# A feed-forward kernel whose gate and up products go from three 256-column steps to one of 512 and one of 256

## The chip, the cores and the metric

The kernel runs on one core of one Trainium2 chip. The metric is the device time of one execution in microseconds (us). TensorE multiplies, VectorE and ScalarE do the elementwise work, SyncE issues the weight transfers, GpSimd a few small ones.

## The reference, cut to what matters

A transformer stack over 256 tokens of 1024 channels, all in float32: a first block with four kinds of token mixing and a feed-forward network, then a second block of two layers, one with a short convolution and one with differential attention, each followed by a feed-forward network and a gated per-layer embedding. The change lies in the three feed-forward networks. The first is

```python
def conv_glu_ffn(h, w_up, conv_w, conv_b, w_down):
    u = causal_dwconv(h @ w_up, conv_w) + conv_b
    gate, up = jnp.split(u, 2, axis=-1)
    return (jax.nn.silu(gate) * up) @ w_down
```

where h is an RMS norm of x, the convolution has 3 taps along the tokens, and gate and up have 2816 channels each. The other two are the same without the bias, and their result is normalised before it is added to x.

## The kernel before, in words

**Precision.** Every float32 operand of a large product is split in two float32r parts: ScalarE rounds it (the high part), VectorE subtracts that from the original (the low part). A product is then the sum of three: high weights by high activations, high weights by low activations, low weights by high activations. The activations of a feed-forward stage are h_hi and h_lo, 8 chunks of 128 channels by 256 tokens.

**Weights.** They come as a stream of 161 blocks of 128 x 2048 elements (1 MB) in the order of use. The ring has 3 slots. For block n SyncE loads raw (once the low part of block n - 3 is made), ScalarE writes w_hi (once TensorE has used block n - 3, whose slot it takes: `act.wait_ge(block_used, n - 2)`), VectorE writes w_lo. `ahead(n)` splits block n + 2. All four engines have their order written out by hand, and wait for each other by counting semaphores.

**A feed-forward stage** (FFN 0, 1, 2; `ffn(f, p)` on each engine) has 33 blocks, called b0 to b32 here. The 2816 hidden channels are done in 11 pairs of 128-channel tiles. Pair q has a gate block, an up block and a down block:

- b0, b1: gate 0 and up 0 (written chunk by chunk as h arrives, `columns_by_chunk`, banks 4 and 5); b2, b3: gate 1, up 1 (banks 6, 7); b4, b5: gate 2, up 2 (banks 4, 5); b6: down 0
- then in a loop of four, two pairs each (`triple`): b7, b8: gate 3, up 3, b9: down 1; b10, b11: gate 4, up 4, b12: down 2; and so on to b28, b29 (gate 10, up 10) and b30 (down 8); at the end b31, b32: down 9 and down 10.

A gate or up block (`columns`) is 48 products: for each of 2 tiles and 8 chunks the three products above, 256 columns each, so that a block's result fills one PSUM bank (2 x 256 columns). The pairs take turns: odd ones use banks 6 and 7, even ones 4 and 5. Banks 0 to 3 hold the sum of the down products (`channel_rows`, 48 products a block). In `triple` TensorE waits for `gate_read` of the pair two before (same bank), for `up_read` likewise, and for `hidden_split` before the down block.

**What VectorE and ScalarE do for pair q.** VectorE reads the gate bank, multiplied by the norm's factor r_x (`read`, L2375, 128 x 512 in one instruction); ScalarE makes the last tap of the convolution (L1536, twice, with a bias in FFN 0 alone); VectorE adds the two older taps (L2357, L2361, twice each); ScalarE takes SiLU (L1545). Up goes the same way without SiLU. VectorE multiplies the two to `hidden` (L2389), ScalarE makes its high part (L1551, `hid_part`), VectorE its low part (L2393), which is `hidden_split`. In the loop VectorE's order is: w_lo of the down block, read gate, taps, w_lo of the next gate block, read up, taps, hidden, w_lo of the next up block, low part of hidden. ScalarE's is: w_hi of the down block, last tap of gate, w_hi of the next gate block, SiLU, last tap of up, w_hi of the next up block, high part of hidden. The splits are L1173 (w_hi) and L1782 (w_lo).

At the start of a stage VectorE's order is: read gate 0, split b4, taps, read up 0, split b5, taps and hidden, read gate 1, split b6, low part of hidden 0, taps, read up 1, split b7, taps and hidden, read gate 2, low part of hidden 1, taps, split b8, read up 2, taps and hidden, low part of hidden 2. ScalarE's: split b4, tap of gate 0, split b5, SiLU and tap of up 0, split b6, high part of hidden 0, tap of gate 1, split b7, SiLU and tap of up 1, split b8, high part of hidden 1, and so on.

Behind FFN 0 comes the residual (`add_residual`, L2271) and the next projection; behind FFN 1 and 2 the squares of the result (L1219) and the per-layer embedding.

Of the kernel before, what the change touches and what calls it, by code (L numbers as in the profile page):

```python
# [10 lines left out]
R = mybir.dt.float32r  # L11
# [5 lines left out]
P = 128  # L17
# [58 lines left out]
for _name, _n in (("fox_b_f", 4), ("gdn_dt", 4), ("gdn_a_log", 4), ("fox_on", 64),  # L76
# [18 lines left out]
    "grams": ("decay_logs", "qk_gram", "decay_turned", "m_turned"),  # L95
    "constants": ("eps_set", "ones_set", "zeros"),
# [9 lines left out]
def build(nc, weights, small_in, x_in, masks_in, ident_in, channel_in, row_in, w_gk_in, p_in, table_in,  # L106
          onehot_in, flip_in, out):
    bias_dram = nc.dram_tensor("bias_by_distance", (N_HEADS, N_DIST), F, kind="Internal").ap()
    with ExitStack() as ctx:
# [16 lines left out]
        h_hi = sb("h_hi", [P, KC, TOK], R)  # L126
        h_lo = sb("h_lo", [P, KC, TOK], R)
# [114 lines left out]
        hidden = place([P, 2, TOK])  # L242
        y_scaled = (y_gate, y_up, z_gate, z_up)
# [152 lines left out]
        def _(pool):  # L396
# [18 lines left out]
            pool.wait_ge(sem("bias_rows"), 1)  # L415
# [11 lines left out]
        def _(pe):  # L427
# [7 lines left out]
            def columns(n0, slot, bank, operand, channel_major=True, middle=(), chunks=None):  # L435
# [4 lines left out]
                for f in range(2):  # L440
# [3 lines left out]
                    for k in range(KC):  # L444
# [9 lines left out]
                        else:  # L454
# [6 lines left out]
                            last = mm(o, a_lo[:, k, tok], ws_hi, False, k == KC - 1)  # L461
                last.then_inc(block_used, 1)
# [513 lines left out]
            def ffn(f, p):  # L976
# [43 lines left out]
            for j in range(4):  # L1020
                n = STEP["sc_out"] + j
                if j == 3:
                    pe.wait_ge(sem("table_loaded"), 32)
                    pe.wait_ge(sem("sc_gc"), 4)
                    mm(PS[0:N_HEADS, 5, 0:N_DIST], table, onehot).then_inc(sem("bias_by_head"), 1)
# [37 lines left out]
            last.then_inc(sem("bias_flipped"), 1)  # L1063
# [12 lines left out]
            def turn_weights(h):  # L1076

                if h == 0:
                    pe.wait_ge(sem("bias_copied"), 1)
# [76 lines left out]
        def _(act):  # L1156
# [365 lines left out]
            def ffn(f, p):  # L1522
# [15 lines left out]

                def gate(q):
# [41 lines left out]
                up(2)  # L1581
# [28 lines left out]
            act.wait_ge(sem("bias_by_head"), 1)  # L1610
# [1163 lines left out]
```

## Time and profile before

| | |
|---|---|
| median of 3 runs | 1098.3 us (1098.29 to 1100.12) |
| the profiled execution | 1100.87 us, span 1099.1 us |
| TensorE matmul | 1063.6 us busy (97%), 9090 instructions |
| VectorE | 804.0 us (73%) |
| ScalarE | 595.6 us (54%) |
| mean granted TensorE clock | 0.992 |
| read from memory | 172.2 MB, 158 GB/s over the span |

The matmul records overlap (one lasts 0.28 us and the next starts 0.12 us later), so the pace is read from start to start, or from the chain of waits. The granted clock is 1.00 at 2.4 GHz and 0.50 at 1.2 GHz. FFN 0 runs from about 212 to 404 us, FFN 1 from 505 to 697 and FFN 2 from 860 to 1053.

### The profile page before, as it was taken

Reading aid. Unit: us, or ns where it says so; the run is one execution under the profiler, and the core shown is the slowest. Engines: PE = TensorE matmul, PEld = TensorE weight load, DVE = VectorE, ACT = ScalarE, POOL = GpSimd, SP = SyncE. Lnnn points to the kernel's source line nnn. Section 1 sums busy time; section 2 is a strip of 40 time slices with the busy share of each in tenths; the row PEclk is TensorE's granted clock in tenths of the full one; section 3 lists DMA queues with packets and bytes.
Section 4 is the critical chain, followed back from the end, with each engine's and each line's share of the span. In section 5 each row is a group of like instructions: output and inputs, shape, how many; then the busy total and the mean of one; then the engine's idle time right before and its main releaser. Section 6 shows DMA issues by size and latency. Waiting matters only on the chain.

```text
span 1099.1 us, 22114 instructions
## 1 busy us (share of the span) xinstructions
PE 1063.6 (97%) x9090; PEld 1039.6 (95%) x9090; DVE 804.0 (73%) x1129; ACT 595.6 (54%) x781; POOL 5.3 (0%) x15
## 2 busy tenths in 40 slices
PE   6999999999999999999999999999998999999996
PEld 6999998999999999998999999989998899999995
DVE  5965678777877786757978777778763787877775
ACT  6652446465555464445555545676665555454563
POOL 0000000000000000000000000000000000000000
PEclk9999999999999999999999999999999999999998
DMA  8421232454555545553655554445343255555431
GB/s 327 156 78 39 78 119 93 150 195 151 191 189 188 195 155 187 183 201 121 202 186 177 194 194 168 154 154 167 141 154 114 92 187 184 193 189 191 153 115 39
DMA packets 25714, 174.23 MB, mean 159 GB/s; under 512 B 3069, under 2 KB 3349, under 8 KB 5296
## 3 DMA queue, kind: packets, MB, share of 16 engines
q1 hardware_dynamic: 25088, 171.57, 45.1%
q0 software_dynamic: 560, 1.70, 0.5%
q8 instruction: 51, 0.84, 0.3%
q14 instruction: 15, 0.12, 0.0%
HBM read 172.20 MB, written 1.06 MB: 158 GB/s over the span
## 4 chain that ended last, share of the span: by engine, by line
PE 71%; DVE 7%; ACT 3%; issue 2%; DVEq 0%; ACTq 0%
PE PS L429 39%; PE PS L466 32%; DVE w_lo L1782 3%; ACT w_hi L1173 2%; DVE arena L2357 1%; ACT arena L1536 1%; DVE arena L2361 1%; DVE arena L2375 1%; DVE x L2304 0%; PE PS L1087 0%; DVE arena L2298 0%; DVE h_lo L1795 0%; DVE arena L2300 0%; DVE arena L2389 0%; DVE arena L2350 0%
## 5 line engine op out<-in xcount | busy, mean ns | idle before, releaser
L1782 DVE TENSOR_TENSOR w_lo<-raw,w_hi 128x2048 fp32r<-128x2048 f32 x158 | 361.1, 2287 | 69.8 <-ACT w_hi L1173 68.1
L429 PE MATMUL PS<-h_hi,w_hi 128*128 128x256 f32 x1248 | 355.5, 285 | 2.6 <-DVE w_lo L1782 2.5
L429 PE MATMUL PS<-h_lo,w_hi 128*128 128x256 f32 x1248 | 353.1, 283 | 0.0
L429 PE MATMUL PS<-h_hi,w_lo 128*128 128x256 f32 x1248 | 353.1, 283 | 0.0
L1173 ACT ACTIVATE w_hi<-raw 128x2048 fp32r<-128x2048 f32 x158 | 300.7, 1905 | 86.2 <-PE PS L466 45.5
L429 PEld LDWEIGHTS PS<-h_hi,w_hi 128*128 128x128 f32 x1248 | 239.3, 192 | 4.3 <-issue 3.9
L429 PEld LDWEIGHTS PS<-h_lo,w_hi 128*128 128x128 f32 x1248 | 239.3, 192 | 0.3 <-issue 0.2
L429 PEld LDWEIGHTS PS<-h_hi,w_lo 128*128 128x128 f32 x1248 | 239.4, 192 | 0.0
L466 PE MATMUL PS<-act_hi,w_hi 128*128 128x256 f32 x720 | 202.2, 282 | 1.2 <-DVE act_lo L1812 1.2
L466 PE MATMUL PS<-act_hi,w_lo 128*128 128x256 f32 x720 | 202.3, 282 | 0.0
L466 PE MATMUL PS<-act_lo,w_hi 128*128 128x256 f32 x720 | 199.7, 283 | 0.0
L1536 ACT ACTIVATE arena<-arena,channel 128x256 f32<-128x256 f32 x132 | 63.9, 531 | 153.4 <-DVE arena L2375 153.4
L466 PEld LDWEIGHTS PS<-act_hi,w_hi 128*128 128x128 f32 x720 | 136.6, 190 | 2.7 <-DVE act_lo L1812 1.4
L466 PEld LDWEIGHTS PS<-act_hi,w_lo 128*128 128x128 f32 x720 | 135.2, 188 | 0.1
L466 PEld LDWEIGHTS PS<-act_lo,w_hi 128*128 128x128 f32 x720 | 133.5, 188 | 0.2
L466 PE MATMUL PS<-h_hi,w_hi 128*128 128x256 f32 (+1 forms) x344 | 97.7, 296 | 17.5 <-ACT h_hi L1190 14.2
L2357 DVE SCALAR_TENSOR_TENSOR arena<-arena,channel 128x255 f32<-128x255 f32 x132 | 58.0, 480 | 69.1 <-ACT arena L1536 69.1
L466 PE MATMUL PS<-h_hi,w_lo 128*128 128x256 f32 (+1 forms) x344 | 95.9, 291 | 0.0
L466 PEld LDWEIGHTS PS<-h_hi,w_hi 128*128 128x128 f32 (+1 forms) x344 | 67.9, 197 | 20.0 <-issue 10.5
L466 PE MATMUL PS<-h_lo,w_hi 128*128 128x256 f32 (+1 forms) x344 | 81.5, 291 | 0.2
L429 PE MATMUL PS<-arena 64*64 64x64 f32 (+8 forms) x1018 | 68.7, 256 | 2.9 <-DVE arena L2157 1.7
L429 PEld LDWEIGHTS PS<-arena 64*64 64x64 f32 (+7 forms) x1018 | 58.8, 155 | 10.9 <-issue 4.5
(304 smaller groups left out, 1304.0 us busy)
## 6 DMA issues: line engine op xcount, KB each, us to landing
raw<-weights SPq DMA_DIRECT2D x158, 1024.0 KB, 4.9
arena<-masks_in SPq DMA_DIRECT2D x1, 1856.0 KB, 14.7
raw<-weights SPq DMA_DIRECT2D x2, 512.0 KB, 5.9
x<-x_in SPq DMA_DIRECT2D x4, 256.0 KB, 7.4
arena<-bias_by_distance POOLq DMA_DIRECT2D x1, 1024.0 KB, 6.2
result<-x SPq DMA_DIRECT2D x4, 256.0 KB, 2.1
arena<-p_in POOLq DMA_DIRECT2D x2, 256.0 KB, 4.2
row<-row_in SPq DMA_DIRECT2D x1, 326.0 KB, 10.8
```

Source lines behind the costliest of these rows:

```text
L429: return pe.matmul(o, lhs, rhs, start=start, stop=stop)
L466: return pe.matmul(o, lhs, rhs, start=start, stop=stop, skip_group_check=True)
L1173: act.activation(w_hi[:, slot, :], raw[:, slot, :], ACT.Copy).then_inc(hi_ready, 1)
L1536: ins = act.activation(dst[:, c, :], src[:, c, :], ACT.Identity, scale=w, bias=b)
L1782: tt(w_lo[:, slot, :], raw[:, slot, :], w_hi[:, slot, :].bitcast(F), ALU.subtract).then_inc(lo_ready, 1)
L2357: stt(y[:, c, 1:TOK], src[:, c, 0:TOK - 1], channel[:, bass.ds(col(1) + c, 1)], y[:, c, 1:TOK], ALU.mult, ALU.add).then_inc(ready[0], 1)
L2361: ins = stt(y[:, c, 2:TOK], src[:, c, 0:TOK - 2], channel[:, bass.ds(col(0) + c, 1)], y[:, c, 2:TOK], ALU.mult, ALU.add)
L2375: tt(z, pair(bank), units(r_x[:, 0:TOK], 2), ALU.mult).then_inc(done, 1)
```

## The change

In the gate and up blocks of pairs 1 to 10 the high and low activations lie side by side, and the high weights are multiplied by both in one product of 512 columns; the low weights by the high activations are added to the first half. A tile thus fills one bank and a block two banks: columns 0 to 255 hold two of the three sums, columns 256 to 511 the third. All gate blocks use banks 6 and 7, all up blocks 4 and 5. ScalarE copies the second halves of both banks to `low` in SBUF (128 x 512), VectorE adds them to the first halves (128 x 512), and then multiplies by r_x. There is one buffer `low` for gate and up. Pair 0 keeps the old form; its up bank is read right behind its gate bank. The layout of h and TensorE's part come first below. Some semaphores used once are shared (`once`), to make room for `low_copied` and `parts_added`.

```diff
-        h_hi = sb("h_hi", [P, KC, TOK], R)
-        h_lo = sb("h_lo", [P, KC, TOK], R)
+        h_both = sb("h_both", [P, KC, 2, TOK], R)
+        h_hi, h_lo = h_both[:, :, 0, :], h_both[:, :, 1, :]
...
+        low = place([P, 2, TOK])
...
+            def wide_columns(n0, slot, bank):
+                block_ready(n0)
+                for f in range(2):
+                    o = PS[:, bank + f, :]
+                    for k in range(KC):
+                        at = k * 256 + f * P
+                        add(o, w_hi[:, slot, at:at + P], h_both[:, k, :, :].rearrange("p b n -> p (b n)"), k == 0)
+                        last = add(o[:, 0:TOK], w_lo[:, slot, at:at + P], h_hi[:, k, :], False, k == KC - 1)
+                last.then_inc(block_used, 1)
...
-                columns(n0 + 2, slot(2), 6, (h_hi, h_lo))
-                columns(n0 + 3, slot(3), 7, (h_hi, h_lo))
+                wide_columns(n0 + 2, slot(2), 6)
+                pe.wait_ge(sem("gate_read"), PAIRS * f + 1)
+                pe.wait_ge(sem("up_read"), PAIRS * f + 1)
+                wide_columns(n0 + 3, slot(3), 4)
...
-                    bank = 6 if odd else 4
-                    pe.wait_ge(sem("gate_read"), pairs_done)
-                    columns(n, slot(at), bank, (h_hi, h_lo))
-                    pe.wait_ge(sem("up_read"), pairs_done)
-                    columns(n + 1, slot(at + 1), bank + 1, (h_hi, h_lo))
+                    pe.wait_ge(sem("gate_read"), pairs_done + 1)
+                    wide_columns(n, slot(at), 6)
+                    pe.wait_ge(sem("up_read"), pairs_done + 1)
+                    wide_columns(n + 1, slot(at + 1), 4)
```

On ScalarE:

```diff
+                def low_part(bank, n_used, q, part):
+                    act.wait_ge(block_used, n_used)
+                    if part or not isinstance(q, int) or q > 1:
+                        act.wait_ge(sem("parts_added"), 2 * q + (2 * (PAIRS - 1) * f + part - 2))
+                    act.activation(low, PS[:, bank:bank + 2, TOK:512], ACT.Copy).then_inc(sem("low_copied"), 1)
...
-                def up(q):
+                def up(q, n_used=None):
                     act.wait_ge(sem("gate_convolved"), q + (PAIRS * f + 1))
                     act.activation(s_gate, y_gate, ACT.Silu).then_inc(sem("gate_silu"), 1)
+                    if n_used is not None:
+                        low_part(4, n_used, q, 1)
                     act.wait_ge(sem("up_read"), q + (PAIRS * f + 1))
...
                     split_of(n_base + 2, step, i)
+                    low_part(6, n_base + 1 + step * i, q, 0)
                     gate(q)
                     split_of(n_base + 3, step, i)
-                    up(q)
+                    up(q, n_base + 2 + step * i)
...
                 hid_part(0, 0)
+                low_part(6, n0 + 3, 1, 0)
                 gate(1)
                 ahead(n0 + 5)
-                up(1)
+                up(1, n0 + 4)
                 ahead(n0 + 6)
+                low_part(6, n0 + 5, 2, 0)
                 hid_part(1, 1)
```

On VectorE:

```diff
+                def read_wide(z, bank, done, q, n_used, part):
+                    dve.wait_ge(block_used, n_used)
+                    dve.wait_ge(sem("low_copied"), 2 * q + (2 * (PAIRS - 1) * f + part - 1))
+                    tt(z, PS[:, bank:bank + 2, 0:TOK], low, ALU.add).then_inc(sem("parts_added"), 1)
+                    dve.wait_ge(sem("parts_added"), 2 * q + (2 * (PAIRS - 1) * f + part - 1))
+                    tt(z, z, units(r_x[:, 0:TOK], 2), ALU.mult).then_inc(done, 1)
+                    dve.wait_ge(done, q + (PAIRS * f + 1))
...
                 read(z_gate, 4, sem("gate_read"), 0, n0 + 1)
+                read(z_up, 5, sem("up_read"), 0, n0 + 2)
                 ahead(n0 + 2)
                 gate(0)
-                read(z_up, 5, sem("up_read"), 0, n0 + 2)
...
-                read(z_gate, 6, sem("gate_read"), 1, n0 + 3)
+                read_wide(z_gate, 6, sem("gate_read"), 1, n0 + 3, 0)
```

All further reads of the stage become `read_wide` in their places, with bank 6 for gate and 4 for up.

## Rows read from the trace of the kernel before

**Rows 1.** Busy time by stretch: us, then busy (instructions) of each engine, PEclk, DMA
```profile
247.40:277.45 30.05, 28.98 (x241) 28.62 (x239) 22.23 (x31) 16.26 (x18) 0.00 (x0) 1.00 0.41 137
277.45:387.00 109.55, 109.55 (x913) 109.55 (x914) 82.97 (x98) 56.95 (x59) 0.00 (x0) 1.00 0.55 192
```
**Rows 2.** Chain that ended last, in order of time: start, us, what
```profile
224.32 23.05 PE PS L429 x192
...
387.08 11.53 PE PS L466 x96
...
405.01 12.13 PE PS L466 x96
...
680.17 15.85 PE PS L466 x132
```
**Rows 3.** Timeline of VectorE, FFN 0: start, us, instruction, idle before it
```profile
261.80 2.29 DVE L1782 TENSOR_TENSOR w_lo<-raw,w_hi 128x2048 fp32r<-128x2048 f32 x1 [1.11 <-ACT w_hi L1173]
264.00 0.68 DVE L2375 TENSOR_TENSOR arena<-PS,arena 128x512 f32<-128x512 f32 x1
266.29 0.88 DVE L2357 SCALAR_TENSOR_TENSOR arena<-arena,channel 128x255 f32<-128x255 f32 x2 [1.60 <-ACT arena L1536]
...
270.31 0.68 DVE L2375 TENSOR_TENSOR arena<-PS,arena 128x512 f32<-128x512 f32 x1
...
277.22 0.68 DVE L2393 TENSOR_TENSOR act_lo<-arena,act_hi 128x512 fp32r<-128x512 f32 x1
...
280.02 0.68 DVE L2375 TENSOR_TENSOR arena<-PS,arena 128x512 f32<-128x512 f32 x1
```
**Rows 4.** Timeline of VectorE, FFN 1, the reads L2375
```profile
557.59 0.69 DVE L2375 TENSOR_TENSOR arena<-PS,arena 128x512 f32<-128x512 f32 x1
...
563.62 0.68 DVE L2375 TENSOR_TENSOR arena<-PS,arena 128x512 f32<-128x512 f32 x1
...
573.12 0.68 DVE L2375 TENSOR_TENSOR arena<-PS,arena 128x512 f32<-128x512 f32 x1
```
**Rows 5.** Timeline of TensorE: first and last of five products of 512 columns
```profile
59.69 0.38 PE L466 MATMUL PS<-gd_hi,level_masks 128*128 128x512 f32 x1
...
60.57 0.38 PE L466 MATMUL PS<-gd_lo,level_masks 128*128 128x512 f32 x1
```
**Rows 6.** Timeline of VectorE, two additions, the second waiting for the first
```profile
215.65 0.68 DVE L1802 TENSOR_TENSOR arena<-xn 128x512 f32<-128x512 f32 x1
216.36 0.69 DVE L1804 TENSOR_TENSOR arena<-arena,xn 128x512 f32<-128x512 f32 x1
```
**Rows 7.** Timeline of ScalarE, a read of 512 columns from PSUM
```profile
694.61 0.60 ACT L1219 ACTIVATE xn<-PS 128x512 f32<-128x512 f32 x1 [0.42 <-PE PS L466]
```
**Rows 8.** Timeline of VectorE, start and end of FFN 0
```profile
227.47 0.68 DVE L2375 TENSOR_TENSOR arena<-PS,arena 128x512 f32<-128x512 f32 x1
...
236.87 0.69 DVE L2389 TENSOR_TENSOR arena<-arena 128x512 f32<-128x512 f32 x1
237.48 0.68 DVE L2375 TENSOR_TENSOR arena<-PS,arena 128x512 f32<-128x512 f32 x1
...
248.35 0.68 DVE L2375 TENSOR_TENSOR arena<-PS,arena 128x512 f32<-128x512 f32 x1
...
400.07 0.75 DVE L2271 TENSOR_TENSOR x<-x,PS 128x256 f32<-128x256 f32 x2 [1.01 <-PE PS L466]
```
**Rows 9.** Busy time by stretch, behind the short convolution; columns as in rows 1
```profile
501.00:517.70 16.70, 14.34 (x102) 14.04 (x103) 13.33 (x25) 9.59 (x16) 0.00 (x0) 0.90 0.30 94
...
502.00:503.00 1.00, 0.00 (x0) 0.00 (x0) 0.96 (x3) 0.30 (x1) 0.00 (x0) 1.00 0.88 156
...
505.00:506.00 1.00, 1.00 (x8) 1.00 (x7) 1.00 (x3) 0.72 (x2) 0.00 (x0) 0.59 0.28 115
```
**Rows 10.** Timeline of ScalarE, start of FFN 0
```profile
241.69 1.92 ACT L1173 ACTIVATE w_hi<-raw 128x2048 fp32r<-128x2048 f32 x1 [2.34 <-PE PS L429]
243.51 0.61 ACT L1545 ACTIVATE arena<-arena 128x512 f32<-128x512 f32 x1
```

More of the change, by code:

```diff
@@ L95 @@
     "grams": ("decay_logs", "qk_gram", "decay_turned", "m_turned"),
+    "bias_by_act": ("bias_rows", "bias_copied", "lambda_exps"),
+    "bias_by_pe": ("bias_by_head", "bias_flipped"),
     "constants": ("eps_set", "ones_set", "zeros"),
@@ L414, in _ @@
             pool.dma_start(p_tok, p_in[0]).then_inc(sem("p_loaded"), 16)
-            pool.wait_ge(sem("bias_rows"), 1)
+            pool.wait_ge(*once("bias_rows"))
             pool.dma_start(bias_dram, bias_row).then_inc(sem("bias_stored"), 16)
@@ L1024, in _ @@
                     pe.wait_ge(sem("sc_gc"), 4)
-                    mm(PS[0:N_HEADS, 5, 0:N_DIST], table, onehot).then_inc(sem("bias_by_head"), 1)
+                    mm(PS[0:N_HEADS, 5, 0:N_DIST], table, onehot).then_inc(once("bias_by_head")[0], 1)
                 pe.wait_ge(sem("sc_hidden"), j + 1)
@@ L1062, in _ @@
                 last = mm(PS[:, b, :], flip, bias_rev[:, 2 * b:2 * b + 2, :].rearrange("p h n -> p (h n)"))
-            last.then_inc(sem("bias_flipped"), 1)
+            last.then_inc(once("bias_flipped")[0], 1)
             def logits(h):
@@ L1078, in turn_weights @@
                 if h == 0:
-                    pe.wait_ge(sem("bias_copied"), 1)
+                    pe.wait_ge(*once("bias_copied"))
                 if h == 6:
@@ L1580, in ffn @@
                 gate(2)
-                up(2)
+                up(2, n0 + 6)
                 act.wait_ge(block_used, n0 + 7)
@@ L1609, in _ @@
                 ahead(STEP["sc_out"] + j)
-            act.wait_ge(sem("bias_by_head"), 1)
-            act.activation(bias_row, PS[0:N_HEADS, 5, 0:N_DIST], ACT.Copy).then_inc(sem("bias_rows"), 1)
+            act.wait_ge(*once("bias_by_head"))
+            act.activation(bias_row, PS[0:N_HEADS, 5, 0:N_DIST], ACT.Copy).then_inc(once("bias_rows")[0], 1)
             squares_of_y(2, 0, STEP["sc_out"] + 4)
@@ L1701, in _ @@
             ahead(a0 + 2)
-            act.wait_ge(sem("bias_flipped"), 1)
-            act.activation(flat(bias_t), PS[:, 0:4, :].rearrange("p b n -> p (b n)"), ACT.Copy).then_inc(sem("bias_copied"), 1)
+            act.wait_ge(*once("bias_flipped"))
+            act.activation(flat(bias_t), PS[:, 0:4, :].rearrange("p b n -> p (b n)"), ACT.Copy).then_inc(once("bias_copied")[0], 1)
             act.wait_ge(sem("lambda_sums"), 1)
-            act.activation(lam[:, 0:2], lam[:, 0:2], ACT.Exp).then_inc(sem("lambda_exps"), 1)
+            act.activation(lam[:, 0:2], lam[:, 0:2], ACT.Exp).then_inc(once("lambda_exps")[0], 1)
             ahead(a0 + 3)
@@ L2395, in triple @@
                 def triple(q, n_base, step, i, odd):
-                    bank = 6 if odd else 4
                     split_of(n_base + 2, step, i)
-                    read(z_gate, bank, sem("gate_read"), q, n_base + 1 + step * i)
+                    read_wide(z_gate, 6, sem("gate_read"), q, n_base + 1 + step * i, 0)
                     gate(q)
                     split_of(n_base + 3, step, i)
-                    read(z_up, bank + 1, sem("up_read"), q, n_base + 2 + step * i)
+                    read_wide(z_up, 4, sem("up_read"), q, n_base + 2 + step * i, 1)
                     up(q)
@@ L2419, in ffn @@
                 gate(1)
-                read(z_up, 7, sem("up_read"), 1, n0 + 4)
+                read_wide(z_up, 4, sem("up_read"), 1, n0 + 4, 1)
                 ahead(n0 + 5)
                 up(1)
-                read(z_gate, 4, sem("gate_read"), 2, n0 + 5)
+                read_wide(z_gate, 6, sem("gate_read"), 2, n0 + 5, 0)
                 hid_part(1, 1)
@@ L2429, in ffn @@
                 ahead(n0 + 6)
-                read(z_up, 5, sem("up_read"), 2, n0 + 6)
+                read_wide(z_up, 4, sem("up_read"), 2, n0 + 6, 1)
                 up(2)
@@ L2531, in lambda_minus @@
             def lambda_minus():
-                dve.wait_ge(sem("lambda_exps"), 1)
+                dve.wait_ge(*once("lambda_exps"))
                 link(tt(lam[:, 2:3], lam[:, 1:2], lam[:, 0:1], ALU.subtract))
@@ L2556, in head @@
                 if h == 0:
-                    dve.wait_ge(sem("bias_copied"), 1)
+                    dve.wait_ge(*once("bias_copied"))
                 for m in range(2):
```

## The prediction

> **What bounds the kernel now.** I read the busy table by stretch first [rows 1]. In the first feed-forward stage (FFN 0) TensorE is busy all the time from 277.45 to 387.00 us; VectorE works 82.97 of those 109.55 us and ScalarE 56.95. A block of 48 products is 5.76 us (96 of them took 11.53 [rows 2], 120 ns each), and a lap (one pair's gate block, up block and one down block) 17.28 us of TensorE. So in the steady part TensorE sets the time, and VectorE, with 13.1 us of work in a lap, seems to have 24% to spare. From 247.40 to 277.45 it is different: TensorE idles only 1.07 us, but VectorE shows waits of its own. There it is catching up, and its reads of gate 3 and gate 4 start 16.02 us apart [rows 3] while TensorE needs 17.28. This is the number that matters most: 16.0 us is the length of VectorE's lap when TensorE doesn't hold it up. It is longer than its 13.1 us of work, because inside a lap it waits twice for ScalarE's last taps (once 1.60 us, at 266.29). In FFN 1, where the tap has no bias, the lap is 15.53 us (557.59 to 573.12 [rows 4]). The cover over VectorE's chain is thus 1.3 us a lap in FFN 0 and 1.7 in FFN 1 and 2, not 4.
>
> **TensorE's part.** Sixty blocks (20 in each of three FFNs; pair 0 keeps the old form) change from 48 products of 256 columns to 16 of 512 and 16 of 256. The columns streamed are the same number; 16 starts are saved. Four steps between 512-column products take 60.57 - 59.69 = 0.88 us, 220 ns each [rows 5], where a 256-column one takes 120. A block goes from 5.76 to 16 x (220 + 120) = 5.44 us. If TensorE stayed the bound: 60 x 0.32 = 19.2 us saved, lap 17.28 - 0.64 = 16.64. Bounds: 16 x (213 + 120) = 5.33, if 512 columns at the granted 2.4 GHz (213 ns) cost nothing else, and 5.76, no gain, at twice the 256-column step. I take the row of the same width. The Trainium skill (TensorE: Matmul & The Clock Gate, Back-to-back issue gap) gives N/2.4 + 2.5 ns, 216 ns for 512 columns and 109 for 256; the rows show 220 and 120, and by the rule a block would take 5.20 us. Neither matters if VectorE takes over.
>
> **VectorE's lap.** Each wide block is read in two steps in place of one: add bank halves to ScalarE's copy, wait for that on its own semaphore, multiply. The multiply costs what the read did. The add is one more 128x512 operation; two such, the second waiting for the first, start 0.71 us apart [rows 6]. I take 0.72; the lower bound is 0.61 (back to back without a wait, 236.87 to 237.48 [rows 8]), the upper 0.87 if the two register-fed waits ahead of it show. Two adds make 1.44 us: the lap becomes 16.0 + 1.44 = 17.44 us in FFN 0 and 15.53 + 1.44 = 16.97 in FFN 1 and 2. Both are above 16.64. VectorE becomes the bound, and TensorE waits for w_lo of the up block, 0.3 to 0.8 us a lap. The copies are in time in this regime: ScalarE reads 512 columns from PSUM in 0.60 us [rows 7], two copies a lap take it from 57 to about 65 of 109.55 us busy, the up copy fits behind SiLU while VectorE splits the next gate block, and the gate copy behind the split of the next down block.
>
> **The start of each FFN.** Here lies most of the price. All wide gate blocks now use banks 6 and 7 and all wide up blocks 4 and 5, so block b4 (gate 2) may not start before gate 1 is read, b5 (up 2) not before up 1 is read. Before, these had banks of their own. VectorE's order puts these reads late. In the clock of FFN 0:
> Up 0 is read right behind gate 0 (227.47 [rows 8]) in place of after gate 0's taps: moved, not added, and b3 finds bank 4 and 5 read at 228.9. The product of pair 0 is made at 236.87 as before. ScalarE queues hid_part(0) (0.54) and then the copy (0.60) behind it, so the add starts at 237.46 + 0.05 + 1.2 = 238.8, the multiply ends at 240.2. TensorE, which starts b2 at 224.3 [rows 2], finished b3 at 224.3 + 2 x 5.44 = 235.2: it idles 5.0 us.
> b4 would run to 245.7. To that comes the clock. In the 16.70 us from 501.00 TensorE was busy for 14.34, with nothing in 502 to 503, so it stood still 2.4 us; the mean granted clock there was 0.90, which is 3.3 us at 0.50 (1.2 GHz), and it fell in 505 to 506 (0.59), after the work had resumed [rows 9]. 3.3 us at half speed lose some 1.6 us of streaming, and an idle twice as long should lose more: I take 2.0, the bounds are 0 and 3.2. End of b4: 247.7.
> Now ScalarE's queue: the split of b7 waits for b4, whose slot it takes (before at 241.69, when b4 ended, then SiLU [rows 10]). 1.9 for the split, 0.55 SiLU, 0.6 copy of up 1, only then VectorE's add and multiply, 1.4: b5 may start at 252.2. A second idle of 4.5 us, again with 2.0 for the clock; b5 ends at 259.7. ScalarE then splits b8 (1.9), copies gate 2 (0.6), VectorE adds and starts to multiply (0.7): 263.0. Before, gate 2 was read at 248.35.
> From there to the read of gate 3 it was 264.00 - 248.35 = 15.65 us [rows 8, 3]; two more adds make it 17.1, less 1.0 because the wait for a w_hi split (1.11 at 261.80 [rows 3]) has gone, TensorE being far ahead of it: gate 3's multiply at 279.1, 15.1 us late. Without the clock's part it would be 11.1.
> The Trainium skill (Perfetto Trace Analysis, Matmuls, under Optimizing Tensor Performance) speaks against this change in the same lines that speak for it: larger products are more efficient, but independent groups should rotate through different PSUM banks so that reading one overlaps the next. The trace before agrees as far as it can: with four rotating banks TensorE stands still 1.07 us from 247.40 to 277.45 [rows 1]. By the half on larger products alone the sum would be -19.2 us.
>
> **Steady part and tail.** FFN 0: pair 10's gate is multiplied at 279.1 + 7 x 17.44 = 401.2. Behind it the last down block needs pair 10's hidden_split: 0.72 (the up's add) + 6.31 (264.00 to 270.31, gate to up) + 6.91 (270.31 to 277.22, up to hidden's low part [rows 3]) + 0.68 = 14.6 us, then 5.76: end at 421.6. Before: 387.08 + 3 x 5.76 = 404.4 [rows 2]. That is +17.2. The next projection waits for VectorE's split of b34, the second block behind this FFN: it started at 405.01 [rows 2], 0.6 us after the end and 4.9 after the residual's first update (400.07 [rows 8]). Now that update waits for b33's split, which comes some 3.3 us behind the last hidden low part (ScalarE's table load and its own split of 1.9 are ahead of it, an estimate): 401.2 + 14.6 + 3.3 + 4.9 = 424.0, +19.0 for FFN 0 in all.
> FFN 1: gate 3 was read at 557.59, now 572.7; + 7 x 16.97 = 691.5. Tail: 0.72 + 6.03 (557.59 to 563.62) + 6.70 (the 6.91 less the 0.21 by which 563.62 to 573.12 is shorter than 270.31 to 280.02 [rows 3, 4]) + 0.68 + 5.76 = 19.9: 711.4, against 680.17 + 17.28 = 697.45 [rows 2]. +13.9. Behind it the squares follow the banks as before, nothing added. FFN 2 the same.
> Sum: 19.0 + 2 x 13.9 = 46.8 us. The profiled execution took 1100.87 us (span 1099.1), which gives 1147.7; the median of the runs is 1098.3, 2.6 lower, which gives 1145.1 us. The h_hi/h_lo layout and the shared semaphores (bias_by_act, bias_by_pe) move no instruction, and a 256-column operand stays contiguous: nothing, and no cover is needed.
>
> **Rivals.**
> (a) As the main case, but the clock stays up: 6 x 2.0 = 12 us less, 1133. For it: [rows 9] is one case, and the clock fell only 2 us after the work had resumed. Against: both idles are twice as long as the one that did it.
> (b) The stalls cost more: 3.2 us for the clock in each of six (+7), and the register-fed waits show, 0.15 on each add (7 laps x 2 x 3 x 0.15 = +6): 1158. For it: the idle of 1.60 us at 266.29, in the loop, is longer than the two taps that it waits for. Against: VectorE's sequencer can run ahead during a 2.28 us split.
> (c) The start hides: TensorE is let go earlier than I read the queue, and only six adds (4.3 us) shift gate 3. FFN 0: +4.3 + 7 x (17.44 - 17.28) - 2.6 (the last gate's read to the end: 23.0 before, 20.4 now) + 1.8 = +4.6; FFN 1, 2: 4.3 - 7 x 0.31 - 3.1 = -1.0 each: 1101. Against: the waits are in the code (gate_read at pairs_done + 1), and the copy stands behind hid_part(0).
> (d) The other side: TensorE stays the bound and the product's saving shows, 1098.3 - 19.2 = 1079. One mechanism decides: VectorE's lap below 16.64, that is an add that costs under 0.32 us in FFN 0 (0.55 in FFN 1, 2), or a VectorE that reads the bank earlier. A 128x512 operation takes 0.68 us in every row, so the row speaks against it, and the start's idles would have to vanish too.
> That the change doesn't do what it says is no case: banks, copies and products are all in the diff.
>
> **How the numbers follow.** Main (as summed, 1139 to 1151): 0.50. (a) 0.15. (b) 0.26. (c) 0.05. (d) 0.04. Predicted time 1145. The range runs from below (a), 1128 (adds at the lower bound, 0.11 x 42 = 4.6 less), to 1162 above (b); with the cases outside it 0.15 stay out. A measurement of this kernel tells some 0.2% (2.2 us) from nothing. Faster: (d), 0.04; same: part of (c), 0.02; slower: 0.94.
>
> **What would show it.** TensorE idle before b4 and b5 of each FFN, 4 to 5 us each, released by the multiply behind read_wide, with PEclk at 0.50 soon after; steps of 220 ns between 512-column products; gate multiplies 17.4 us apart in FFN 0 and 17.0 in FFN 1 and 2; TensorE waiting for w_lo once a lap; last down block ending 17 us late in FFN 0 and 14 in the others. I am wrong if the idles before b4 and b5 are under 2 us (then (c)), if the lap is 16.6 (then (d)), or if ScalarE's copies come late in the steady loop, which would lengthen the lap beyond 18.

## The result, and the profile after

The changed kernel takes 1150.7 us (median of 4 runs, 1149.69 to 1150.97) against 1099.0 us before (4 runs): a ratio of 1.0465, 95% interval 1.0453 to 1.0478. It is slower by 51.7 us. The profiled execution took 1150.97 us (span 1149.2), 50.1 us more than the span of before. The mean granted clock fell from 0.992 to 0.977.

The page of the changed kernel, TensorE, VectorE and ScalarE:

```profile
PE 1072.8 (93%) x8130; PEld 1000.1 (87%) x8130; DVE 843.6 (73%) x1189; ACT 626.8 (55%) x841; POOL 5.3 (0%) x15
```

960 products fewer, 40 us more of VectorE, and TensorE no longer busy for 97% of the span but for 93%. What it waits for (us in total, times, longest):

```profile
PE PS L481 <- DVE arena L2412: 27.7, 6, 4.6
PE PS L481 <- DVE w_lo L1810: 16.3, 16, 2.4
```

L2412 is the multiply in `read_wide`, L1810 the split w_lo. The six waits are b4 and b5 of each FFN. Of the sixteen for w_lo, ten are in or right around FFN 0 and three each in the first laps of FFN 1 and FFN 2. In FFN 0 TensorE's idles, from its timeline between 233 and 300 us:

```profile
240.43 0.79 PE L481 MATMUL PS<-h_both,w_hi 128*128 128x512 f32 x1 [4.63 <-DVE arena L2412]
253.66 0.80 PE L481 MATMUL PS<-h_both,w_hi 128*128 128x512 f32 x1 [4.58 <-DVE arena L2412]
280.14 0.36 PE L481 MATMUL PS<-act_hi,w_hi 128*128 128x256 f32 x1 [2.39 <-DVE w_lo L1810]
```

The third idle is before b9. What VectorE did meanwhile, to be read against [rows 3, 8]:

```profile
238.96 0.69 DVE L2410 TENSOR_TENSOR arena<-PS,arena 128x512 f32<-128x512 f32 x1 [1.25 <-ACT arena L1560]
239.68 0.69 DVE L2412 TENSOR_TENSOR arena<-arena 128x512 f32<-128x512 f32 x1
...
252.19 0.69 DVE L2410 TENSOR_TENSOR arena<-PS,arena 128x512 f32<-128x512 f32 x1 [7.18 <-ACT arena L1560]
252.91 0.69 DVE L2412 TENSOR_TENSOR arena<-arena 128x512 f32<-128x512 f32 x1
...
263.49 0.69 DVE L2410 TENSOR_TENSOR arena<-PS,arena 128x512 f32<-128x512 f32 x1 [5.13 <-ACT arena L1560]
264.22 0.69 DVE L2412 TENSOR_TENSOR arena<-arena 128x512 f32<-128x512 f32 x1
...
280.63 0.69 DVE L2412 TENSOR_TENSOR arena<-arena 128x512 f32<-128x512 f32 x1
...
298.02 0.69 DVE L2412 TENSOR_TENSOR arena<-arena 128x512 f32<-128x512 f32 x1
```

These are gate 1, up 1, gate 2, gate 3 and gate 4. Gate 3's multiply was at 264.00 before and is 16.6 us later; from there a lap is 17.39 us. VectorE waited 7.18 us for a copy (L1560) that itself takes 0.58. ScalarE's queue says why (compare [rows 10]):

```profile
249.17 1.91 ACT L1189 ACTIVATE w_hi<-raw 128x2048 fp32r<-128x2048 f32 x1 [7.67 <-PE PS L481]
250.99 0.61 ACT L1568 ACTIVATE arena<-arena 128x512 f32<-128x512 f32 x1
251.51 0.58 ACT L1560 ACTIVATE arena<-PS 128x512 f32<-128x512 f32 x1
```

The copy of up 1, whose bank was full since 235.8, stands behind the split of b7, which takes b4's slot and so waits for the end of b4. TensorE can't start b5 before up 1 is copied and read, so b4 (TensorE), the split, SiLU and the copy (ScalarE), the add and the multiply (VectorE) and b5 come strictly one after the other. The chain of FFN 0 has both blocks:

```profile
240.43 8.66 PE PS L481 x32
...
253.66 7.25 PE PS L481 x32
...
425.02 5.03 PE PS L481 x40
```

At full clock this row of the chain is 5.93 us for a wide block (experiment 3 below); these took 8.66 and 7.25. (The row runs to the end of the last product; from its first start to the next block's a wide block is 5.65 us here.) The last row is the next projection, which started at 405.01 before [rows 2]: 20.0 us later. The windows show the clock (columns as in rows 1):

```profile
240.00:246.00 6.00, 5.57 (x17) 4.80 (x18) 4.94 (x7) 1.09 (x2) 0.00 (x0) 0.50 0.38 109
...
254.00:256.00 2.00, 2.00 (x7) 1.72 (x7) 2.00 (x2) 0.73 (x2) 0.00 (x0) 0.50 0.00 0
...
281.00:284.00 3.00, 3.00 (x16) 3.00 (x16) 1.34 (x4) 2.49 (x3) 0.00 (x0) 0.50 0.92 322
```

After each of the three idles the granted clock is 0.50 (1.2 GHz) for some microseconds in which TensorE is busy. Its pace in b3, at full clock (start, us):

```profile
232.81 0.40 PE L481 MATMUL PS<-h_both,w_hi 128*128 128x512 f32 x1
233.05 0.28 PE L481 MATMUL PS<-h_both,w_lo 128*128 128x256 f32 x1
233.16 0.40 PE L481 MATMUL PS<-h_both,w_hi 128*128 128x512 f32 x1
```

512 and 256 columns together take 233.16 - 232.81 = 0.35 us where three times 256 took 0.36.

FFN 1 and FFN 2 are different from FFN 0 behind the start. TensorE waits for w_lo the last time at 606.89 (b11); from there its row in the chain has no gap up to the end of FFN 1:

```profile
606.89 0.47 PE L481 MATMUL PS<-h_both,w_hi 128*128 128x512 f32 x1 [1.63 <-DVE w_lo L1810]
```

```profile
606.89 118.84 PE PS L481 x800
```

Its down blocks b12 to b30 start at 612.60 to 714.06, six laps of 16.91 us, and VectorE's laps there are 16.9 too: the two engines are level, and both are below the 17.28 us of before. FFN 2 is the same from 978.57 on.

### The profile page after: what moved, and what is told of

The parts are those of the page before. It is cut to its first block, busy times and chain, and to the rows that moved or that the text cites. A ratio compares the mean times of both kernels' runs of the same rounds, so it can differ in the third digit from the quotient of the medians.

```text
span 1149.2 us, 20482 instructions
## 1 busy us (share of the span) xinstructions
PE 1072.8 (93%) x8130; PEld 1000.1 (87%) x8130; DVE 843.6 (73%) x1189; ACT 626.8 (55%) x841; POOL 5.3 (0%) x15
## 4 chain that ended last, share of the span: by engine, by line
PE 53%; DVE 17%; issue 8%; ACT 5%; DVEq 1%; ACTq 0%
PE PS L481 41%; PE PS L432 11%; DVE w_lo L1810 7%; DVE arena L2412 2%; DVE arena L2410 2%; ACT arena L1552 2%; DVE arena L2385 2%; DVE arena L2389 1%; ACT w_hi L1189 1%; DVE act_lo L2430 1%; DVE x L2332 0%; ACT arena L1560 0%; PE PS L1103 0%; DVE arena L2326 0%; DVE arena L2426 0%
## 5 line engine op out<-in xcount | busy, mean ns | idle before, releaser
L481 PE MATMUL PS<-h_both,w_hi 128*128 128x512 f32 (+2 forms) x1648 | 485.3, 360 | 53.6 <-DVE arena L2412 27.7
L1810 DVE TENSOR_TENSOR w_lo<-raw,w_hi 128x2048 fp32r<-128x2048 f32 x158 | 361.0, 2287 | 60.9 <-ACT w_hi L1189 59.8
L481 PEld LDWEIGHTS PS<-h_both,w_hi 128*128 128x128 f32 (+1 forms) x1648 | 298.1, 196 | 104.9 <-DVE arena L2412 29.6
L481 PE MATMUL PS<-h_both,w_lo 128*128 128x256 f32 (+1 forms) x1304 | 370.6, 287 | 0.0
L481 PEld LDWEIGHTS PS<-h_both,w_lo 128*128 128x128 f32 (+1 forms) x1304 | 256.1, 196 | 0.2
L432 PE MATMUL PS<-h_both,w_hi 128*128 128x256 f32 x576 | 105.5, 285 | 0.0
L432 PEld LDWEIGHTS PS<-h_both,w_hi 128*128 128x128 f32 x576 | 89.8, 192 | 0.9 <-issue 0.5
L432 PE MATMUL PS<-h_both,w_lo 128*128 128x256 f32 x288 | 81.4, 283 | 0.0
L2410 DVE TENSOR_TENSOR arena<-PS,arena 128x512 f32<-128x512 f32 x60 | 41.1, 684 | 41.7 <-ACT arena L1560 41.7
L2389 DVE SCALAR_TENSOR_TENSOR arena<-arena,channel 128x254 f32<-128x254 f32 x132 | 57.9, 480 | 7.6 <-DVE arena L2385 0.3
L432 PE MATMUL PS<-w_hi,h_both 128*128 128x256 f32 x288 | 55.7, 287 | 0.0
```

The costliest lines, as they stand in the source:

```text
L432: return pe.matmul(o, lhs, rhs, start=start, stop=stop)
L481: return pe.matmul(o, lhs, rhs, start=start, stop=stop, skip_group_check=True)
L1810: tt(w_lo[:, slot, :], raw[:, slot, :], w_hi[:, slot, :].bitcast(F), ALU.subtract).then_inc(lo_ready, 1)
L2389: ins = stt(y[:, c, 2:TOK], src[:, c, 0:TOK - 2], channel[:, bass.ds(col(0) + c, 1)], y[:, c, 2:TOK], ALU.mult, ALU.add)
L2410: tt(z, PS[:, bank:bank + 2, 0:TOK], low, ALU.add).then_inc(sem("parts_added"), 1)
```

## The experiments

Theory: the price is paid at the start of each FFN, where the shared banks make TensorE wait for reads whose copies stand late in ScalarE's queue, and where the idles cost clock on top; in the loop VectorE's lap is the bound, and the product itself saves little. Rivals: VectorE's larger amount of work costs it everywhere; the products themselves, or the clock, are the main price; the shared banks alone are.

**1. Old start, new loop** (`x1_old_start`). Pairs 1 and 2 as before, `read_wide` and wide products from pair 3 on.

```diff
-                wide_columns(n0 + 2, slot(2), 6)
+                columns(n0 + 2, slot(2), 6, (h_hi, h_lo))
+                columns(n0 + 3, slot(3), 7, (h_hi, h_lo))
...
-                read_wide(z_gate, 6, sem("gate_read"), 1, n0 + 3, 0)
+                read(z_gate, 6, sem("gate_read"), 1, n0 + 3)
```

> The changed kernel with the old products, banks and order for pairs 1 and 2, the wide form only in the loop (pairs 3 to 10). Theory A (the price is the start of each FFN, where shared banks meet copies that stand late in ScalarE's queue; the adds only lengthen VectorE's lap to 17.4 and 16.9 us): gate 3 is read at 264.7 in FFN 0, end of FFN 0 at 406.8 (+2.4), the next projection +4, FFN 1 and 2 each -1: 1101 us. Rival B (VectorE's added work is the price wherever it stands, 16 of the 20 reads a stage are left): still about 1140. Rival C (the wide products or the clock in the loop cost it): 1130 or more.

Measured: 1102.3 us, ratio 1.0028 (1.0018 to 1.0038). Each series of runs has its own runs of the kernel before (median 1099.0 for the changed kernel, 1099.9 here); against those, 49.3 of the 51.7 us are gone. VectorE's multiplies of gates 3 and 4 in FFN 0:

```profile
263.72 0.69 DVE L2414 TENSOR_TENSOR arena<-arena 128x512 f32<-128x512 f32 x1
...
281.11 0.69 DVE L2414 TENSOR_TENSOR arena<-arena 128x512 f32<-128x512 f32 x1
```

Gate 3 is back at its old time, and the lap is 17.39 us as in the changed kernel. So the wide loop as a whole costs 2.4 us; the start costs the rest. The loop doesn't cost it evenly: from b2 to the next b2 (from the last one, to the end) FFN 0, with its longer lap, takes 3.8 us more than before, and FFN 1 and FFN 2, whose laps are shorter than before, 0.8 us less each.

**2. The wide start in a better order** (`x2_mended_start`). All is wide, in the shared banks; only the copies and reads of gate 1, up 1 and gate 2 move ahead in their queues, before the split that waits for the same block of TensorE or a later one.

```diff
                 ahead(n0 + 3)
-                up(0)
-                ahead(n0 + 4)
-                hid_part(0, 0)
                 low_part(6, n0 + 3, 1, 0)
-                gate(1)
-                ahead(n0 + 5)
-                up(1, n0 + 4)
-                ahead(n0 + 6)
-                low_part(6, n0 + 5, 2, 0)
-                hid_part(1, 1)
+                up(0)
+                low_part(4, n0 + 4, 1, 1)
+                ahead(n0 + 4)
+                hid_part(0, 0)
+                gate(1)
+                low_part(6, n0 + 5, 2, 0)
+                ahead(n0 + 5)
+                up(1)
+                ahead(n0 + 6)
+                hid_part(1, 1)
```

VectorE's `read_wide` calls move with them.

> The changed kernel, all as wide, only the order at the start of each FFN altered: ScalarE copies gate 1 before SiLU of pair 0 and up 1 right behind the last tap of up 0, copies gate 2 before it splits b7; VectorE reads gate 1, up 1 and gate 2 one place earlier. Theory A: TensorE no longer idles before b4 and b5, the clock stays up, gate 3 is multiplied at about 266.5 in place of 280.6: 14 us less in each FFN, 1109 us. Rival B (amount of VectorE's work, which is unchanged here): 1150. Rival D (the shared banks alone stall TensorE whatever the order): 1135 to 1150.

Measured: 1110.5 us, ratio 1.0104 (1.0082 to 1.0126), mean clock 0.991. TensorE's waits:

```profile
PE PS L481 <- DVE w_lo L1811: 15.5, 15, 2.6
...
PE PS L481 <- DVE arena L2413: 1.6, 3, 0.6
```

The multiply (L2413 here) made it wait 27.7 us in the changed kernel and 1.6 now; the w_lo waits stay. With the same banks, products, copies and adds, 40.2 us go by order alone. The banks alone are not the price.

**3. The clock alone** (`x3_keep_busy`). The changed kernel, with products into bank 3, which holds nothing yet, in TensorE's two waits of each FFN.

```diff
+                    if first:
+                        keep_busy(19)
                     pe.wait_ge(sem("gate_read"), pairs_done + 1)
                     wide_columns(n, slot(at), 6)
+                    if first:
+                        keep_busy(18)
                     pe.wait_ge(sem("up_read"), pairs_done + 1)
```

> The changed kernel with 19 products of 512 columns (h by h, into bank 3, which nobody reads) before TensorE's wait ahead of b4 and 18 ahead of b5, in each FFN: the wait is as long, but TensorE isn't idle in it. Theory A: b4 takes 5.65 us in place of 8.7 and b5 5.65 in place of 7.3, 4.7 us less in each FFN: 1136.5 us; the idle of 2.4 us ahead of b9 and its drop of the clock may stay, in VectorE's shadow. Rival (the clock costs nothing, since VectorE sets the lap anyway): 1150. Rival (the clock is the main price): below 1125.

Measured: 1135.0 us, ratio 1.0321 (1.0298 to 1.0344), so 15.7 us of the 51.7 are the clock's, 2.6 for each of the six idles (16.6 if each kernel is set against the before of its own series). The window of b4, and its row in the chain:

```profile
240.00:246.00 6.00, 5.86 (x33) 5.12 (x34) 4.65 (x7) 1.09 (x2) 0.00 (x0) 1.00 0.40 128
```

```profile
240.14 5.93 PE PS L481 x32
```

b4 starts 0.3 us from where it did (240.43 in the changed kernel), the clock is 1.00 in place of 0.50, and 8.66 us become 5.93. The waits for the reads are as long as before and cost the other 24.5 us (40.2 - 15.7) of the start's order.

**4. The adds alone** (`x4_old_plus_op`). Old products, banks and order, and one more 128x512 operation on VectorE behind each read of pairs 1 to 10 (it adds zeros).

```diff
-                    tt(z, PS[:, bank:bank + 2, 0:TOK], low, ALU.add).then_inc(sem("parts_added"), 1)
+                    tt(z, pair(bank), units(r_x[:, 0:TOK], 2), ALU.mult).then_inc(sem("parts_added"), 1)
...
-                    tt(z, z, units(r_x[:, 0:TOK], 2), ALU.mult).then_inc(done, 1)
+                    tt(z, z, zeros_r.bitcast(F).rearrange("p (c n) -> p c n", c=2), ALU.add).then_inc(done, 1)
```

> The kernel before (old products, banks and order, no copies on ScalarE) with one more VectorE operation per read of pairs 1 to 10, 128x512, adding zeros, behind a wait on its own semaphore, as the add of the changed kernel. Theory A: six operations (4.3 us) delay gate 3's read; the lap is 17.39 us in FFN 0, in FFN 1 and 2 TensorE's 17.28 stays the bound: FFN 0 +7.5 with the next projection, the others +3 each: 1112 us. Rival B (VectorE's added work is the price): 1145 to 1150.

Measured: 1111.7 us, ratio 1.0116 (1.0094 to 1.0138). VectorE's reads of gates 4 and 5:

```profile
283.52 0.68 DVE L2409 TENSOR_TENSOR arena<-PS,arena 128x512 f32<-128x512 f32 x1
...
300.94 0.69 DVE L2409 TENSOR_TENSOR arena<-PS,arena 128x512 f32<-128x512 f32 x1
```

One operation a read makes the lap of FFN 0 17.42 us, and the kernel 11.8 us slower, with nothing else changed. It is within 1.2 us of experiment 2, which has the wide products and the copies besides. That is a balance and doesn't show that the products do nothing: in FFN 1 the down blocks come every 17.27 us here, at TensorE's old pace, and every 16.93 in experiment 2, but experiment 2 waits longer before b9 (2.4 to 2.6 us against 1.4 to 1.6).

**5. Without the adds** (`x5_no_add`). The changed kernel without copies and adds: `read_wide` only multiplies. In pairs 1 to 10 it leaves out high weights by low activations in the sum, though TensorE still computes it.

```diff
-                    tt(z, PS[:, bank:bank + 2, 0:TOK], low, ALU.add).then_inc(sem("parts_added"), 1)
...
-                    tt(z, z, units(r_x[:, 0:TOK], 2), ALU.mult).then_inc(done, 1)
+                    tt(z, PS[:, bank:bank + 2, 0:TOK], units(r_x[:, 0:TOK], 2), ALU.mult).then_inc(done, 1)
```

> The changed kernel without ScalarE's copies and without VectorE's adds (left out of the computation: the high weights by the low activations in pairs 1 to 10); the wide products and the shared banks stay. VectorE's lap is 16.0 and 15.5 us, TensorE's 2 x 5.65 + 5.76 = 17.06. Theory A: TensorE still waits for the read of gate 1 (2.8 us, the clock then drops for some 3.4 us), not for up 1; in the loop it is the bound and gains 0.22 us a lap: about 2 us over before in each FFN, 1104 us. Rival (the banks alone stall TensorE in every lap): 1120 or more. Rival (the wide product would pay at once without the add): 1085 to 1092.

Measured: 1102.3 us, ratio 1.0028 (1.0019 to 1.0037). With every add gone it is still 2.6 us slower than before:

```profile
PE PS L481 <- DVE arena L2405: 7.7, 3, 2.6
PE PS L481 <- DVE w_lo L1806: 4.2, 8, 1.0
```

L2405 is the read of gate 1, once in each FFN: this is what the shared banks cost when nothing else is late. I had expected 1104, with a block that saves 0.11 us as read at b2 and b3; experiment 9 shows about 0.2 in the loop.

**6 and 7. A new order in VectorE's loop** (`x6_mended_reordered`, `x7_old_start_reordered`). Inside a lap VectorE split w_lo of the down block, read the gate and then stood idle for ScalarE's last tap (1.51 us at 282.83; in the kernel before it was 1.60 [rows 3]). Read first, and the split hides the tap:

```diff
-                    split_of(n_base + 2, step, i)
                     read_wide(z_gate, 6, sem("gate_read"), q, n_base + 1 + step * i, 0)
+                    split_of(n_base + 2, step, i)
                     gate(q)
```

Experiment 6 is this on the mended start of experiment 2, and with b9's split ahead of the loop:

> All wide, the start as in the kernel with the mended start, and in the loop VectorE splits the down block between the read of the gate and its taps, where it waited 1.5 us for ScalarE; the split of b9 comes before the loop, in the wait for up 2's tap. Theory A: VectorE's lap is 15.9 us in FFN 0, TensorE (17.06) is the bound again but for some 3 us of waits around b9 to b11: 1097 us. Rival (VectorE's amount of work sets the lap whatever the order): 1108 to 1111, as the mended start alone.

Measured: 1096.6 us, ratio 0.9973 (0.9963 to 0.9982). Experiment 7 is this on the old start of experiment 1:

> The old form for pairs 1 and 2, the wide form in the loop, and the same order in the loop (down block's split between the read of the gate and its taps). Theory A: TensorE's bound of 17.06 us a lap with some 1.5 us of waits at the first lap: 1.7 us less than before in each FFN, 1094.5 us, 0.5% faster than before. Rival (no gain is left in the wide product): 1099 or more.

Measured: 1095.6 us, ratio 0.9966 (0.9953 to 0.9980). Both are 0.3% faster than the kernel before, and both within 1.1 us of what I expected. That alone would have made a good story about wide products. It needed a control.

**8. The control: the kernel before with that order and nothing else** (`x8_before_reordered`).

```diff
-                    split_of(n_base + 2, step, i)
                     read(z_gate, bank, sem("gate_read"), q, n_base + 1 + step * i)
+                    split_of(n_base + 2, step, i)
                     gate(q)
```

> The kernel before with that one order in VectorE's loop (down block's split between the read of the gate and its taps), no wide product. Theory A: TensorE's lap of 17.28 us is the bound before and after, only the 1.1 us idle ahead of the first laps can change: 1099, the same within 0.2%. Rival (a faster time of the reordered wide kernel comes from the order, not from the product): 1095.

Measured: 1095.8 us, ratio 0.9964 (0.9951 to 0.9976). My expectation fell: the order alone gives the whole gain of experiment 7. The runs of the two lie between 1094.1 and 1097.1 us and between 1094.3 and 1100.6, so a gain or loss of a microsecond or two by the product can't be told from them. In its chain, FFN 0 from b2 on:

```profile
224.56 23.03 PE PS L429 x192
247.59 5.76 PE PS L466 x48
253.35 11.51 PE PS L429 x96
264.87 5.76 PE PS L466 x48
```

TensorE runs without a gap where it had stood still 1.07 us before 277.45 [rows 1]. I had taken the small waits of the kernel before as no more than noise; TensorE's waits for w_lo were 2.9 us in all there and are 0.4 here. In the trace of experiment 7 TensorE waits before b9, 2.06 us in FFN 0 and 2.2 in FFN 1 and FFN 2. In FFN 1:

```profile
560.88 0.55 PE L481 MATMUL PS<-act_hi,w_hi 128*128 128x256 f32 x1 [2.21 <-DVE w_lo L1812]
```

All its waits for w_lo, 8.4 us against 0.4 in the control, take back most of what the wide products save. The profiled execution took 1100.6 us, 5 more than the median, and in it the clock fell behind each of the three waits.

**9 and 10. That wait taken away, beside the control** (`x9_split_early`, `x10_before_reordered_again`). Experiment 7 with the two parts of b9 made before pair 2's last up taps:

```diff
-                up(2)
+                up(2, None, n0 + 7)
...
                 read(z_up, 5, sem("up_read"), 2, n0 + 6)
+                ahead(n0 + 7)
                 up(2)
```

Pairs 3 and 4 are written out in front of the loop, so that pair 3 can leave that split out.

> The kernel with the old start and the new order in VectorE's loop, with one more move: the two parts of the first looped down block (b9) are made before pair 2's last up taps, ahead of the loop, and pairs 3 and 4 are written out in front of the loop. In the kernel with the old start TensorE waited 2.2 us in each feed-forward stage for w_lo of that block, right before it. If those waits go and nothing else comes late, the three stages give back 6 us at most, of which VectorE's lap of 17.39 us in FFN 0 (TensorE's own is 17.06) takes about 2.3 back: I expect 1091 to 1092, that is 4 to 5 us below the kernel before with the new order, and TensorE's waits for w_lo in FFN 1 and 2 under 0.5 us. Theory: the product's saving of 0.11 us a block (6.6 us over 60) is there once nothing waits. Rival: the saving isn't there over a whole stage, TensorE waits elsewhere for VectorE, and the time is that of the kernel before with the new order, 1095 to 1096.

> The kernel before with the new order in VectorE's loop, once more, so that it stands beside the one with the wide product on the same chip: 1095.8 again. By the theory it is 4 to 5 us above the kernel with the wide product and the early split, by the rival level with it.

Measured on one chip: 1089.7 us for experiment 9 (5 runs, 1089.51 to 1089.83), ratio to before 0.9917 (0.9903 to 0.9931); 1096.2 us for the control (10 runs), ratio 0.9972 (0.9963 to 0.9982). The wide product in the loop (16 of the 20 blocks of each FFN) is worth 6.5 us, 0.6%, once little hides it; the control's runs lie between 1094.4 and 1097.9. Experiment 9 also has the early split and two pairs written out, which the control has not; but in the control's trace TensorE waits for w_lo for 0.4 us in all, none of it inside an FFN's loop, so an early split has nothing to win there. What the two written-out pairs are worth by themselves no run shows. TensorE's waits for w_lo went from 8.4 us to this:

```profile
PE PS L481 <- DVE w_lo L1817: 3.1, 5, 1.7
```

And its chain in FFN 0 has six laps without a wait:

```profile
275.57 101.42 PE PS L481 x672
```

672 products are six laps of 112; a lap is 101.42 / 6 = 16.90 us, against 17.28 before. A wide block is (16.90 - 5.76) / 2 = 5.57 us, 0.19 less than an old one; VectorE's lap fits below that, in the new order, with both adds in it. The books balance: 48 blocks at 0.19 us are 9.1 us, less 2.7 for TensorE's longer waits for w_lo (3.1 against 0.4), which leaves 6.4.

Experiment 6 has the same loop and the same early split and differs from experiment 9 in the start alone, which is wide there: it is 6.9 us slower, with waits of 0.9 to 1.4 us before b7 and b8 in each FFN. Wide blocks pay in the loop, and in pairs 1 and 2 they cost as much again.

| kernel | us | against before |
|---|---|---|
| changed kernel | 1150.7 | +51.7 |
| 3: clock kept up | 1135.0 | +35.1 |
| 4: before, one more operation a read | 1111.7 | +11.8 |
| 2: mended start | 1110.5 | +10.6 |
| 1: old start | 1102.3 | +2.4 |
| 5: no adds | 1102.3 | +2.6 |
| 6: mended start, new order | 1096.6 | -3.1 |
| 8, 10: before, new order | 1095.8, 1096.2 | -3.9, -3.1 |
| 7: old start, new order | 1095.6 | -4.1 |
| 9: old start, new order, early split | 1089.7 | -9.6 |

## Why the prediction was right, step by step

**Direction and place: right.** The main case held: the idles before b4 and b5, VectorE as the bound in the loop of FFN 0, and the late end of each FFN.

**Size: 5.6 us short, in two parts.** The sum was 46.8 us; the spans differ by 50.1. b2's first product started at 223.97, 517.39 and 873.01 us before and at 224.15, 536.95 and 907.43 after: 0.2 us come before the first, and from one to the next, and from the last to the end of the span, the kernel lost 19.4, 14.9 and 15.7 us, where the sum had 19.0, 13.9 and 13.9. So 3.3 us lie there, most of them in the terms below. The rest is the base: the profiled execution of before was 2.6 us over its median, and I took that off; the changed kernel's profiled execution lay at its median (1150.97 and 1150.72), and before has a median of 1099.0 in the runs beside it, not 1098.3.

**A wide block: mis-sized.** I had 5.44 us, from 220 ns for 512 columns and 120 for 256; measured were 5.65 (b2, b3) and 5.57 (experiment 9). The saving is 0.11 to 0.19 us, not 0.32. The row that I took [rows 5] was one of five equal products in a row, and here a 512-column product stands behind a 256-column one; the alternating step is 0.35 us, by starts 0.24 and 0.11. By the Trainium skill's rule (TensorE: Matmul & The Clock Gate, Back-to-back issue gap), which is given there for a single product and its gap, it would be 0.325, an estimate; no run here comes to that. At the start of an FFN it counts 0.2 us a block, of which b4 came 0.2 us late. In the loop it makes TensorE's own lap 16.9 us, not 16.64.

**VectorE's lap: right; that TensorE waits for it in every lap: right in FFN 0 alone.** 17.44 and 16.97 were predicted, 17.39 and 16.92 measured. In FFN 1:

```profile
593.25 0.69 DVE L2412 TENSOR_TENSOR arena<-arena 128x512 f32<-128x512 f32 x1
...
610.18 0.69 DVE L2412 TENSOR_TENSOR arena<-arena 128x512 f32<-128x512 f32 x1
```

Experiment 4 gives the same lap with the operation alone. That the number to start from was VectorE's lap while it catches up, 16.02 us, and not its 13.1 us of work, was the reading that mattered. In FFN 0 TensorE waits for w_lo of the up block in each lap, as foreseen (0.17 to 0.27 us by the profile, once the first laps are over). In FFN 1 and FFN 2 it doesn't, behind the first lap: its own lap is as long as VectorE's, 16.91 us. That the time of those two stages is VectorE's lap, as the sum had it, is in part luck: without the adds, in experiment 5, the lap of FFN 1 is still 16.86 us.

**The first idle: right.** b4 was predicted at 240.2 after an idle of 5.0; it started at 240.43 after 4.63.

**The clock: mis-sized.** I took 2.0 us each. In FFN 0 b4 lost 8.66 - 5.93 = 2.7 us and b5 7.25 - 5.93 = 1.3. b5 started at 253.66, 1.5 later than I had it: 0.2 was there at b4, 0.7 is clock, and the rest is the block's own time to the end of its last product, 5.93 where I had 5.44. In FFN 1 and FFN 2 the chain has 7.45 and 8.33 us for b4, after idles of the same 4.6 us. Over the six idles experiment 3 measures 15.7 us, 2.6 each, where I had 12. Rival (a), the clock staying up, was worked out as 1133; experiment 3 made it so and measured 1135.0.

**The second idle: right.** 4.5 us predicted, 4.58 measured, by the queue as read: split of b7, SiLU, copy, add, multiply.

**Gate 3: 1.5 us late.** Its multiply came at 280.63, not 279.1. Gate 2's, at 264.22 and not 263.0, carries 1.2 of it; the stretch between the two was 16.41 us, not 16.1. That it came so near is luck. I had 17.1 less 1.0 for a wait for w_hi that would be gone, TensorE being far ahead. The wait is still there, and as long [rows 3]:

```profile
277.70 2.29 DVE L1810 TENSOR_TENSOR w_lo<-raw,w_hi 128x2048 fp32r<-128x2048 f32 x1 [1.11 <-ACT w_hi L1189]
```

That split didn't wait for TensorE, before or after: ScalarE makes it right behind the high part of `hidden` (at 275.24), for which it waits for VectorE (2.72 us). What went instead is another wait, for ScalarE's high part of hidden 1, before the low part. In the kernel before it was

```profile
249.99 0.69 DVE L2393 TENSOR_TENSOR act_lo<-arena,act_hi 128x512 fp32r<-128x512 f32 x1 [0.95 <-ACT act_hi L1551]
```

and in the changed kernel the same instruction, at 264.94, has none.

**Not foreseen: the third idle.** TensorE waited 2.39 us before b9 (2.29 in FFN 1 and FFN 2), and in FFN 0 the clock fell again, to 0.50 from 281 to 284 us. TensorE waits for VectorE once more behind it, 1.57 us before b11, so I count it as nothing in the changed kernel. In experiment 7 TensorE waits no more after b9, and there the idle before it was worth removing.

**The tail: right within 1 us.** The last gate multiply, hidden's low part, b33's split and the residual's first update:

```profile
402.21 0.69 DVE L2412 TENSOR_TENSOR arena<-arena 128x512 f32<-128x512 f32 x1
...
416.05 0.69 DVE L2430 TENSOR_TENSOR act_lo<-arena,act_hi 128x512 fp32r<-128x512 f32 x1
417.93 2.29 DVE L1810 TENSOR_TENSOR w_lo<-raw,w_hi 128x2048 fp32r<-128x2048 f32 x1 [1.19 <-ACT w_hi L1189]
420.13 0.74 DVE L2299 TENSOR_TENSOR x<-x,PS 128x256 f32<-128x256 f32 x2
```

Predicted were 401.2 for the first and 424.0 for the next projection, which started at 425.02; 1.0 of that is carried from the front.

**The rivals.** (b) asked for more clock loss and for 0.15 us on each add; the first was half right (0.6 an idle), the second wrong (two adds made 1.37 to 1.39 us of lap). (c) and (d) fell; (c)'s sum, 1101, is close to experiment 1, where the idles really are gone (1102.3), and so are its parts: +4.6, -1.0 and -1.0 by stage, measured +3.8, -0.8 and -0.8. The rule that independent groups should rotate through PSUM banks (the Trainium skill, Perfetto Trace Analysis, Matmuls under Optimizing Tensor Performance) agrees with experiment 5, where the shared banks alone cost 7.7 us of waits; experiment 2 shows that most of the price in the changed kernel came from the order of the reads behind them.

**Where the gain was.** (d)'s idea, that the larger product pays once VectorE is short enough, was right in kind, at a third of its size: 6.5 us for 48 blocks, not 19.2 for 60. VectorE is short enough for it with the two adds left in, once the split fills the idle for ScalarE's tap inside its lap.

What stays open: why a wide block is 5.65 us at b2 and b3 and shorter in the loop of experiment 9. The changed kernel has both kinds side by side at full clock: in the loop of FFN 0 a 512 and a 256 together take 0.347 us in the gate blocks, before which TensorE didn't wait, and 0.350 in the up blocks, before which it did. Open is also why the clock took 2.7 us from b4 in FFN 0 but 1.3 from b5 after an idle of the same length.

## What to carry to other kernels

Before work is put on an engine that "has 24% to spare", measure its lap where nothing holds it up, waits for its neighbours included; that is its cover. When two products come to share a PSUM bank, follow the read that frees the bank through the queues of every engine it touches, and move it ahead of any instruction that waits for TensorE itself. And when an experiment on the changed kernel beats the old one, apply the same edit to the old one too: here it gave the whole gain of experiment 7, and only the pair of experiments 9 and 10 showed what the change was worth.

## What was not expected of the hardware

- A 512-column float32r product that alternates with a 256-column one takes 0.24 us from start to start, not the 0.22 of equal ones in a row [rows 5]; the pair takes 0.347 to 0.353 us.
- After an idle of 4.6 us the granted clock was 0.50 for 6 us (240 to 246) in one case and for some 2 to 3 us (254 to 256) in the next; after one of 2.39 us, for 3 us (281 to 284). The shorter idle did not cost less than the second long one: b9 took 7.3 us in place of 5.76.
- After the idle of 2.29 us before b9 of FFN 1 (592.76), nearly as long, the clock didn't fall at all:

```profile
592.00:599.00 7.00, 5.99 (x48) 5.81 (x48) 5.54 (x8) 3.83 (x5) 0.00 (x0) 1.00 0.42 151
```
